# In the expert turns, each down unit is multiplied ahead of the transposes of the newest middle tile

## The chip, the core and the metric

The kernel runs on one core of a Trainium2 chip. Its time is the device time of one execution in microseconds (us), as the median of several runs. TensorE (PE in the rows) does the matrix products, its weight loads are shown apart as PEld, VectorE is DVE, ScalarE is ACT, GpSimd is POOL, and SyncE (SP) asks for the loads from HBM. Each engine works through its own instructions in the order in which they were written, and waits at an instruction until the semaphores that it names have come far enough.

## The reference, cut to what matters

The model is two hybrid blocks of two layers each over 256 tokens of width 1024. What the change touches is the last feed-forward part, a mixture of 8 experts with an inner width of 2816, two experts for each token:

```python
def _moe_swiglu(x, w_router, w_gate, w_up, w_down):
    ...
    top_logit, top_idx = lax.top_k(logits, TOP_K)
    top_w = jax.nn.softmax(top_logit, axis=-1)
    ...
    def expert_block(args):
        xs, e = args
        return (jax.nn.silu(xs @ w_gate[e]) * (xs @ w_up[e])) @ w_down[e]
    yb = lax.map(expert_block, (xb, block_expert))
    y_rows = yb.reshape(n_rows, d) * row_weight[:, None].astype(x.dtype)
    out = jnp.zeros_like(xf).at[row_token].add(y_rows)
```

All of it is float32, and the kernel keeps nearly that accuracy.

## The kernel before

**The whole.** Attention block, dense feed-forward, recurrent mixer and so on run first, up to 1510 us of the profiled execution. From there to 2361 us run the expert turns. One turn takes the up to 128 tokens of one expert through its three weight matrices. The program has a first turn written out, a loop of further turns and a last turn written out; with these inputs there are nine turns.

**The units.** An expert's weights come as 33 units of 1 MB, each 128 partitions by 2048 floats. The inner width is cut in 11 middle tiles of 256, j = 0 to 10. Tile j has three units: `near` j and `far` j (the halves of the gate and the up matrix over the model width) and `down` j. The order of the units in the stream is near j, far j, down j-2 for j = 2 to 10 (near and far alone for j = 0 and 1), then down 9 and down 10.

**The split.** A float32 product is made of three products in the faster rounded format. ScalarE copies a loaded unit into its high part (`w_hi`, line 1941), VectorE subtracts it from the unit to get the low part (`w_lo`, line 2962), and TensorE multiplies high by high, high by low and low by high. Each unit is 12 matmuls of 512 columns: line 1348 for near and far, line 1373 for down. A unit waits for its low part (`moe_lo`). High and low parts stand in four buffers, in three late in the turn; the raw units in six slots, later five. SyncE loads a slot anew once the low part of its last unit has been made.

**One middle tile.** When far j is done, ScalarE takes the silu of the gate half (line 1949) and VectorE multiplies it by the up half (line 2971, `moe_hidden`). TensorE then turns this 128 by 256 tile with two transposes (`turn_hidden`, line 1358, into bank 6). ScalarE copies the turned tile to its high part `hT_hi` (line 1924), and VectorE subtracts to get `hT_lo` (line 2956). `down` j needs both, two tiles later.

**What sets the order.** Four lists are written by hand, one for each engine, and share only semaphores. ScalarE and VectorE go through the units with an offset of two: step i makes the high part (VectorE: the low part) of unit i, and then does what belongs to unit i-2. In the step of far j ScalarE does this:

```python
act_(moe_part(w_hi, at), moe_slot(at), ACT.Copy)      # L1941, the unit near j+1
...
act_(act_m[:, j % 2, :], banks[4 + j % 2][:, 0:256], ACT.Silu)
if j:
    hT(j - 1)                                         # L1924; waits for turned_hidden j-1
```

The next high part in ScalarE's list, behind `hT(j-1)`, is that of far j+1, and then come those of down j-1 and near j+2. VectorE's list has the same sequence: hidden j, `hT_lo` j-1, and the low parts of far j+1, down j-1 and near j+2. Some small work of VectorE stands between `hT_lo` and the next low part (finding rows in the first turn, the picks of the next turn), and in the last turn rows of other turns are added (lines 2943 and 2947). Behind down 8 the turns but the last have eight transposes of gathered rows (line 1409), then `turn_hidden(10)`, down 9 and down 10; ScalarE and VectorE make the high and low part of down 10, the parts of the gathered rows, and then `hT` 10.

Of the kernel before, what the change touches and what calls it, by code (L numbers as in the profile page):

```python
# [217 lines left out]
def emit(nc, known, stream, par_d, cst_d, rows_d, x_d, out_d, n_stages):  # L218
# [5 lines left out]
    with ctx:  # L224
# [109 lines left out]
        def ct(name, i=0, n=None):  # L334
            a, w = CST.at[name]
            return cst[:, a + i:a + (w if n is None else i + n)]
# [3 lines left out]
        def sm(name, width):  # L340
            if name not in small_at:
                used = sum(w for _, w in small_at.values())
                assert used + width <= 512
                small_at[name] = (used, width)
            a, w = small_at[name]
            return small[:, a:a + w]
# [407 lines left out]
        def _(pe):  # L754
# [557 lines left out]
            if n_stages == 4:  # L1312
                mixer(1, MIX2_1)
                sel = sm("tables", 6 * 24).rearrange("p (t c) -> p t c", t=6)[:, 0:2, :]
                pe.wait_ge(*V.of("selected"))
                three = banks[1][:, 0:24].rearrange("p (t c) -> p t c", t=3)
                mm(three, ct("earlier"), sm("tables", 6 * 24).rearrange("p (t c) -> p t c", t=6)[:, 0:3, 0:8], start=True, stop=False)
                mm(three[:, 1:3, :], ct("ones"), grow(sel[:, 0, 0:8], [P, 2, 8], 1), start=False, stop=False)
                mm(three[:, 2, :], ct("ones"), sel[:, 1, 0:8], start=False, stop=True).then_inc(*T.done("places"))

                pe.wait_ge(*V.of("pick0"))
                for k in range(KT):
                    for tb in range(TB):
                        r = mm(banks[2 + k // 4][:, (k % 4) * P:(k % 4 + 1) * P], xr[:, tb, k * P:(k + 1) * P],
                               pick[:, tb, :], start=(tb == 0), stop=(tb == TB - 1))
                    if k % 4 == 3:
                        r.then_inc(*T.done("gather0", k // 4))

                def scatter(tb, half):

                    for y in (y_hi, y_lo):
                        r = mm(banks[2 + 4 * tb + half], pickT[:, tb * P:(tb + 1) * P], y[:, half * 512:(half + 1) * 512],
                               start=(y is y_hi), stop=(y is y_lo))
                    return r

                def turn(n, peeled, last=False):
                    where["turn"] = n

                    def up(kind, j):
                        i = MOE_UNIT[(kind, j)]  # L1340
                        if i >= 2:
                            pe.wait_ge(*V.of("moe_lo", i))
                        else:
                            pe.wait_ge(*(V.of("first_lo", i) if peeled else V.before("moe_lo", i)))
                        for q in range(4):
                            k = q + 4 * (kind == "far")
                            for a, b in ((xe_hi, w_hi), (xe_lo, w_hi), (xe_hi, w_lo)):
                                r = mm(banks[4 + j % 2], a[:, k, :], moe_part(b, i)[:, q * 512:(q + 1) * 512],  # L1348
                                       start=(k == 0 and a is xe_hi and b is w_hi), stop=(k == KT - 1 and b is w_lo))
                        r.then_inc(*T.done("moe_unit", i))  # L1350
                        T.same((f"moe_{kind}", j), ("moe_unit", i))

                    def turn_hidden(j):
                        pe.wait_ge(*V.of("moe_hidden", j))
                        if j:
                            pe.wait_ge(*V.of("hT", j - 1))
                        for c in range(2):
                            r = nc.tensor.transpose(banks[6][:, c * P:(c + 1) * P], hid_m[:, j % 2, c * P:(c + 1) * P],  # L1358
                                                    ct("ident"))
                        r.then_inc(*T.done("turned_hidden", j))  # L1360

                    def down(j):
                        i = MOE_UNIT[("down", j)]
                        pe.wait_ge(*V.of("moe_lo", i))
                        pe.wait_ge(*V.of("hT", j))
                        if j == 0:
                            pe.wait_ge(*A.of("y", 1))
                        order = [(c, half) for c in range(2) for half in range(2)]
                        if last and j == FJ - 1:
                            order = [(c, half) for half in range(2) for c in range(2)]  # L1370
                        for c, half in order:
                            for a, b in ((hT_hi, w_hi), (hT_lo, w_hi), (hT_hi, w_lo)):
                                r = mm(banks[half], a[:, j % 2, c * P:(c + 1) * P],  # L1373
                                       moe_part(b, i)[:, c * D + half * 512:c * D + (half + 1) * 512],
                                       start=(j == 0 and c == 0 and a is hT_hi and b is w_hi),
                                       stop=(j == FJ - 1 and c == 1 and b is w_lo))
                            if last and j == FJ - 1 and (c, half) == (1, 0):
                                r.then_inc(*T.done("last_half", 0))
                        r.then_inc(*T.done("moe_unit", i))
                        T.same(("last_half", 1), ("moe_unit", i))  # L1380
                        T.same(("moe_down", j), ("moe_unit", i))

                    for j in range(FJ):
                        if j == 0:
                            pe.wait_ge(*(V.of("xe0", 0) if peeled else V.before("xe", 0)))
                        elif j >= 2:
                            pe.wait_ge(*V.of("moe_hidden", j - 2))
                        up("near", j)
                        if j == 0:
                            pe.wait_ge(*(V.of("xe0", 1) if peeled else V.before("xe", 1)))  # L1390
                        up("far", j)
                        if j:
                            turn_hidden(j - 1)
                        if j >= 2:
                            down(j - 2)
                        if j == 8 and last:
                            pe.wait_ge(*V.of("pickw"))
                            for tb in range(TB):
                                r = nc.tensor.transpose(banks[7][:, tb * P:(tb + 1) * P], pickw[:, tb, :], ct("ident"))
                            r.then_inc(*T.done("pickT"))  # L1400
                        if j == 4 and not last:
                            pe.wait_ge(*V.of("pick"))
                            for tb in range(TB):
                                r = mm(banks[7][:, 256:257], pick[:, tb, :], ct("token", tb, 1), start=(tb == 0), stop=(tb == TB - 1))
                            r.then_inc(*T.done("row_at"))
                    if not last:
                        pe.wait_ge(s_gathered, n * 16 + 16)
                        for k in range(KT):
                            r = nc.tensor.transpose(banks[2 + k // 4][:, (k % 4) * P:(k % 4 + 1) * P],
                                                    turn_rows[:, k * P:(k + 1) * P], ct("ident"))  # L1410
                            if k % 4 == 3:
                                r.then_inc(*T.done("gather", k // 4))
                    turn_hidden(FJ - 1)
                    down(FJ - 2)
                    down(FJ - 1)
                T.enter()
                turn(0, True)
                T.again()
                load_turns(pe)
                with pe.Fori(1, where["turns"]) as n:  # L1420
                    turn(n, False)
                T.leave()
                turn(where["turns"], False, True)
                pe.wait_ge(*V.of("pickT"))
                for half in range(2):
                    pe.wait_ge(*V.of("last_y", half))
                    for tb in range(TB):
                        scatter(tb, half).then_inc(*T.done("last_scattered", tb, half))
# [1899 lines left out]
```

## Time and profile before

| what | value |
|---|---|
| median of 3 runs | 2379.02 us (2376.97 to 2379.52) |
| span of the profiled execution, first to last instruction | 2375.0 us |
| share of the span: PE, DVE, ACT | 98%, 81%, 61% |
| stretch of the expert turns, 1510 to 2351 us: PE busy | 840.4 of 841 us |
| same stretch: DVE, ACT busy | 744.8, 621.9 us |
| same stretch: mean busy share of the DMA engines | 0.97 |

The profiled execution's own time is its span plus what lies around it; the median of the runs is 4.0 us above the span. A busy share says how long an engine had an instruction in work, and not which engine waited for which. For that the timeline is read: each of its rows has the start in us from the span's start, the duration, the engine, the line, the operation and the tiles, how many instructions are merged in it (x), and in brackets how long the engine stood idle before it and what released it. TensorE's granted clock (PEclk) is 1.00 at 2.4 GHz and 0.50 at 1.2 GHz.

### The profile page before, as it was taken

The page shows a single profiled execution, that of the slowest core. Times are in us where ns is not written, and L with a number is a line of the kernel's source. Part 1 is how long each engine was busy: PE and PEld are TensorE (multiplying, and loading weights), DVE is VectorE, ACT ScalarE, POOL GpSimd, SP SyncE. Part 2 cuts the span into 40 slices and gives each one's busy share as a digit, 9 for nine tenths or more (in the row PEclk, how much of TensorE's full clock was granted, in tenths as well). Part 3 has the DMA queues.
Part 4 walks back from the last instruction along what each step waited for, and adds up shares of the span by engine and source line. Part 5 has one row for each costly group of instructions (what it writes and reads, how often), then busy time and mean ns, then how long its engine had stood idle before and what let it go on. Part 6 is the DMA issues. An engine that isn't in the chain of part 4 may idle for free.

```text
span 2375.0 us, 41596 instructions
## 1 busy us (share of the span) xinstructions
PE 2330.6 (98%) x16350; PEld 2040.7 (86%) x16350; DVE 1916.5 (81%) x2378; ACT 1442.3 (61%) x1765; POOL 139.3 (6%) x135
## 2 busy tenths in 40 slices
PE   8999999999999999999999999899999999999997
PEld 8998888999888999888889988788888888888886
DVE  5678877758888689876667887888888888888888
ACT  5765555665655553544446343677767777777775
POOL 2100000400000011100000120000000000000000
PEclk9999999999999999999999999899999999999999
DMA  6455553543655332455544223899999999999996
GB/s 236 162 195 195 195 195 125 189 167 136 224 188 193 141 143 91 161 195 192 189 164 173 108 91 124 343 362 385 384 367 393 361 382 392 359 385 386 368 381 267
DMA packets 83320, 575.23 MB, mean 242 GB/s; under 512 B 9568, under 2 KB 10080, under 8 KB 15840
## 3 DMA queue, kind: packets, MB, share of 16 engines
q1 hardware_dynamic: 78560, 554.21, 61.8%
q0 software_dynamic: 4608, 18.88, 2.0%
q8 instruction: 110, 1.80, 0.3%
q14 instruction: 42, 0.34, 0.0%
HBM read 561.25 MB, written 8.39 MB: 240 GB/s over the span
## 4 chain that ended last, share of the span: by engine, by line
PE 92%; DVE 4%; issue 2%; ACT 1%; DMA 0%; POOL 0%; DVEq 0%; SPq 0%; POOLq 0%; ACTq 0%
PE bank L1348 22%; PE bank L807 16%; PE bank L1373 11%; PE bank L816 9%; PE bank L854 7%; PE bank L818 5%; PE bank L909 4%; PE bank L888 3%; PE bank L1255 3%; PE bank L839 3%; DVE yT L2570 1%; PE bank L1358 1%; PE bank L1157 1%; PE bank L996 1%; DVE ring_lo L2492 0%
## 5 line engine op out<-in xcount | busy, mean ns | idle before, releaser
L2962 DVE TENSOR_TENSOR w_lo<-ring,w_hi 128x2048 fp32r<-128x2048 f32 x214 | 482.5, 2289 | 70.3 <-ACT w_hi L1941 69.0
L1941 ACT ACTIVATE w_hi<-ring 128x2048 fp32r<-128x2048 f32 x214 | 401.7, 1918 | 25.5 <-PE bank L1348 12.8
L1348 PE MATMUL bank<-w_hi,xe_hi 128*128 128x512 f32 x792 | 311.5, 393 | 0.5 <-DVE w_lo L2962 0.5
L1348 PE MATMUL bank<-w_lo,xe_hi 128*128 128x512 f32 x792 | 308.7, 390 | 0.0
L1348 PE MATMUL bank<-w_hi,xe_lo 128*128 128x512 f32 x792 | 308.2, 389 | 0.0
L2029 DVE TENSOR_TENSOR w_lo<-ring,w_hi 128x2048 fp32r<-128x2048 f32 x97 | 222.1, 2291 | 55.0 <-ACT w_hi L1478 53.6
L816 PE MATMUL bank<-x_both,w_hi 128*128 128x512 f32 x960 | 239.9, 392 | 0.0
L1478 ACT ACTIVATE w_hi<-ring 128x2048 fp32r<-128x2048 f32 x99 | 189.7, 1918 | 38.0 <-PE bank L854 34.1
L816 PEld LDWEIGHTS bank<-x_both,w_hi 128*128 128x128 f32 x960 | 174.3, 189 | 32.3
L1348 PEld LDWEIGHTS bank<-w_hi,xe_hi 128*128 128x128 f32 x792 | 148.7, 188 | 34.3 <-DVE w_lo L2962 4.3
L1348 PEld LDWEIGHTS bank<-w_lo,xe_hi 128*128 128x128 f32 x792 | 148.6, 188 | 31.5
L1348 PEld LDWEIGHTS bank<-w_hi,xe_lo 128*128 128x128 f32 x792 | 148.8, 188 | 30.1
L807 PE MATMUL bank<-x_hi,in_hi 128*128 128x256 f32 x576 | 164.3, 285 | 0.0
L1373 PE MATMUL bank<-w_hi,hT_hi 128*128 128x512 f32 x396 | 163.8, 414 | 0.3 <-DVE w_lo L2962 0.2
L807 PE MATMUL bank<-x_hi,ring_lo 128*128 128x256 f32 x576 | 162.3, 282 | 0.0
L807 PE MATMUL bank<-x_lo,in_hi 128*128 128x256 f32 x576 | 161.3, 280 | 0.0
L2156 DVE TENSOR_TENSOR ring_lo<-ring,in_hi 128x2048 fp32r<-128x2048 f32 x39 | 89.4, 2295 | 85.2 <-ACT in_hi L1517 85.1
L1489 ACT ACTIVATE gates<-bank 128x256 f32<-128x256 f32 x120 | 39.6, 382 | 191.4 <-PE bank L818 191.4
L1373 PE MATMUL bank<-w_hi,hT_lo 128*128 128x512 f32 x396 | 155.6, 393 | 0.0
L1373 PE MATMUL bank<-w_lo,hT_hi 128*128 128x512 f32 x396 | 155.0, 391 | 0.0
L1949 ACT ACTIVATE gates<-bank 128x256 f32<-128x256 f32 x99 | 38.0, 384 | 175.6 <-PE bank L1348 175.0
L818 PEld LDWEIGHTS bank<-x_both,w_lo 128*128 128x128 f32 x960 | 131.0, 190 | 9.4
(468 smaller groups left out, 5833.5 us busy)
## 6 DMA issues: line engine op xcount, KB each, us to landing
ring<-in_stream SPq DMA_DIRECT2D x431, 1024.0 KB, 5.4
yT<-in_stream SPq DMA_DIRECT2D x54, 1024.0 KB, 7.7
xT<-in_stream SPq DMA_DIRECT2D x27, 1024.0 KB
Z<-in_stream SPq DMA_DIRECT2D x8, 1024.0 KB, 7.7
norm_rows<-in_rows POOLq DMA_DIRECT2D x4, 1024.0 KB, 7.3
slot_rows<-gates POOLq DMA_DIRECT2D x8, 512.0 KB, 8.9
Z<-Z SPq DMA_DIRECT2D x24, 128.0 KB, 2.1
slot_rows<-cst POOLq DMA_DIRECT2D x4, 512.0 KB, 4.2
```

What stands on the lines that cost most here:

```text
L807: r = mm(bank[:, c * SEQ:(c + 1) * SEQ], w[a][:, at], x[b][:, k, :], start=(k == 0 and a == b), stop=(k == KT - 1 and a == 1))
L816: mm(two[c], w[0][:, at[k]], x_both[:, :, k, :], start=(k == 0), stop=False)
L818: r = mm(two[c][:, SEQ:2 * SEQ], w[1][:, at[k]], x_hi[:, k, :], start=False, stop=(k == KT - 1))
L854: r = mm(banks[2 * tb + half], a[:, j % 2, c, tb * P:(tb + 1) * P], part(b, n)[:, c * D + half * 512:c * D + (half + 1) * 512], start=(j = ...
L909: r = mm(banks[2 * tb + half], g[a], w[:, c, half * 512:(half + 1) * 512], start=(n == 0 and c == 0 and a == b), stop=(n == 3 and c == 1 a ...
L1348: r = mm(banks[4 + j % 2], a[:, k, :], moe_part(b, i)[:, q * 512:(q + 1) * 512], start=(k == 0 and a is xe_hi and b is w_hi), stop=(k == K ...
L1373: r = mm(banks[half], a[:, j % 2, c * P:(c + 1) * P], moe_part(b, i)[:, c * D + half * 512:c * D + (half + 1) * 512], start=(j == 0 and c ...
L1478: act_(part(w_hi, n), slot(f0 + n), ACT.Copy).then_inc(*A.done("hi", f0 + n))
L1941: act_(moe_part(w_hi, at), moe_slot(at), ACT.Copy).then_inc(*A.done("moe_hi", at))
L2029: v.tensor_tensor(part(w_lo, n), slot(f0 + n), part(w_hi, n).bitcast(F32), ALU.subtract)\
L2156: v.tensor_tensor(slot_lo(u), slot(u), hi.bitcast(F32), ALU.subtract).then_inc(*V.done("lo", u))
L2962: v.tensor_tensor(moe_part(w_lo, at), moe_slot(at), moe_part(w_hi, at).bitcast(F32), ALU.subtract)\
```

## The change

In `turn`, for each j from 2 to 10, `down(j - 2)` is called ahead of `turn_hidden(j - 1)` instead of behind it. The number of instructions and the waits that each one carries stay the same.

```diff
                         up("far", j)
+                        if j >= 2:
+                            down(j - 2)
                         if j:
                             turn_hidden(j - 1)
-                        if j >= 2:
-                            down(j - 2)
```

TensorE at j = 2 of the first turn, before. Bank 4 is that of far 2, bank 6 takes the transposes, banks 0 and 1 sum the down units, and bank 5 is that of near 3:

```order
L1348 MATMUL bank4<-w_hi_49,xe_lo_96 128x512
L1348 MATMUL bank4<-w_lo_50,xe_hi_95 128x512
L1358 MATMUL bank6<-cst,gates 128x128 x2
L1373 MATMUL bank0<-w_hi_49,hT_hi_97 128x512
...
L1373 MATMUL bank1<-w_hi_49,hT_hi_97 128x512
L1373 MATMUL bank1<-w_hi_49,hT_lo_98 128x512
L1373 MATMUL bank1<-w_lo_50,hT_hi_97 128x512
L1348 MATMUL bank5<-w_hi_3_54,xe_hi_95 128x512
```

The same place in the changed kernel:

```order
L1348 MATMUL bank4<-w_hi_49,xe_lo_96 128x512
L1348 MATMUL bank4<-w_lo_50,xe_hi_95 128x512
L1373 MATMUL bank0<-w_hi_49,hT_hi_97 128x512
L1373 MATMUL bank0<-w_hi_49,hT_lo_98 128x512
...
L1373 MATMUL bank1<-w_hi_49,hT_lo_98 128x512
L1373 MATMUL bank1<-w_lo_50,hT_hi_97 128x512
L1358 MATMUL bank6<-cst,gates 128x128 x2
L1348 MATMUL bank5<-w_hi_3_54,xe_hi_95 128x512
```

The two transposes moved behind the 12 matmuls of down 0, directly in front of near 3. ScalarE's list is the same in both kernels. Around the copies of turned tiles 1 and 2 it reads (`gates<-bank` is the silu, `hT_hi` the copy of the turned tile):

```order
L1949 ACTIVATE gates<-bank4 128x256
L1924 ACTIVATE hT_hi_97<-bank6 128x256
L1941 ACTIVATE w_hi_49<-ring 128x2048 x2
L1941 ACTIVATE w_hi_49<-yT 128x2048
L1949 ACTIVATE gates<-bank5 128x256
L1924 ACTIVATE hT_hi_97<-bank6 128x256
L1941 ACTIVATE w_hi_3_54<-xT 128x2048
```

The first `w_hi` behind each `hT_hi` is the high part of a far unit: far 3 behind the first, far 4 (from xT) behind the second. Nothing moved here, nor on VectorE, GpSimd or SyncE.

At the end of a turn that is not the last, TensorE reads before:

```order
L1373 MATMUL bank1<-w_lo_50,hT_hi_97 128x512
L1409 MATMUL bank2<-cst,Z 128x128 x4
L1409 MATMUL bank3<-cst,Z 128x128 x4
L1358 MATMUL bank6<-cst,gates 128x128 x2
L1373 MATMUL bank0<-w_hi_49,hT_hi_97 128x512
```

and in the changed kernel:

```order
L1373 MATMUL bank1<-w_lo_50,hT_hi_97 128x512
L1358 MATMUL bank6<-cst,gates 128x128 x2
L1409 MATMUL bank2<-cst,Z 128x128 x4
L1409 MATMUL bank3<-cst,Z 128x128 x4
L1358 MATMUL bank6<-cst,gates 128x128 x2
L1373 MATMUL bank0<-w_hi_49,hT_hi_97 128x512
```

The transposes of tile 9 moved behind down 8, in front of those of the gathered rows.

## Rows read from the trace of the kernel before

**Rows 1.** The page: the span, and the chain that ended last, by engine.

```profile
span 2375.0 us, 41596 instructions
...
PE 92%; DVE 4%; issue 2%; ACT 1%; DMA 0%; POOL 0%; DVEq 0%; SPq 0%; POOLq 0%; ACTq 0%
```

**Rows 2.** Groups by line, 1450 to 2375 us: the transposes of line 1358.

```profile
L1358 PE MATMUL bank<-cst,gates 128*128 128x128 f32 x198 | 37.6, 271 | 0.0
```

**Rows 3.** Waits, 1510 to 2351 us: total us, times, longest.

```profile
ACT gates L1949 <- PE bank L1348: 174.2, 94, 2.9
...
PEld bank L1348 <- DVE w_lo L2962: 4.3, 13, 0.7
```

**Rows 4.** Timeline of TensorE, second turn: transposes, down, near, far, transposes.

```profile
1629.71 0.38 PE L1358 MATMUL bank<-cst,gates 128*128 128x128 f32 x2
1629.85 0.47 PE L1373 MATMUL bank<-w_hi,hT_hi 128*128 128x512 f32 x1
...
1632.70 0.39 PE L1348 MATMUL bank<-w_hi,xe_hi 128*128 128x512 f32 x1
...
1635.42 0.39 PE L1348 MATMUL bank<-w_hi,xe_hi 128*128 128x512 f32 x1
...
1638.14 0.38 PE L1358 MATMUL bank<-cst,gates 128*128 128x128 f32 x2
```

**Rows 5.** Timeline of ScalarE, same stretch: silu, hT, first high part.

```profile
1629.99 0.38 ACT L1949 ACTIVATE gates<-bank 128x256 f32<-128x256 f32 x1 [2.37 <-PE bank L1348]
1630.27 0.38 ACT L1924 ACTIVATE hT_hi<-bank 128x256 fp32r<-128x256 f32 x1
1630.53 1.92 ACT L1941 ACTIVATE w_hi<-xT 128x2048 fp32r<-128x2048 f32 x1
```

**Rows 6.** Timeline of VectorE, same stretch: the three low parts.

```profile
1632.49 2.29 DVE L2962 TENSOR_TENSOR w_lo<-xT,w_hi 128x2048 fp32r<-128x2048 f32 x1 [1.09 <-ACT w_hi L1941]
1634.70 4.49 DVE L2962 TENSOR_TENSOR w_lo<-ring,w_hi 128x2048 fp32r<-128x2048 f32 x2
```

**Rows 7.** Timeline of three engines, end of the last turn.

```profile
2349.91 4.49 DVE L2962 TENSOR_TENSOR w_lo<-ring,w_hi 128x2048 fp32r<-128x2048 f32 x2
...
2352.25 0.50 PE L1373 MATMUL bank<-w_hi,hT_hi 128*128 128x512 f32 x1 [0.17 <-DVE w_lo L2962]
...
2355.12 0.44 PE L1358 MATMUL bank<-cst,gates 128*128 128x128 f32 x2
...
2355.67 0.38 ACT L1924 ACTIVATE hT_hi<-bank 128x256 fp32r<-128x256 f32 x1 [0.82 <-PE bank L1358]
```

**Rows 8.** Timeline, end of the second turn: transposes 9, down 10's start; VectorE.

```profile
1689.26 0.38 PE L1358 MATMUL bank<-cst,gates 128*128 128x128 f32 x2
...
1696.13 0.40 PE L1373 MATMUL bank<-w_hi,hT_hi 128*128 128x512 f32 x1
...
1692.04 2.29 DVE L2962 TENSOR_TENSOR w_lo<-yT,w_hi 128x2048 fp32r<-128x2048 f32 x1 [0.39 <-ACT w_hi L1941]
...
1695.45 0.41 DVE L2956 TENSOR_TENSOR hT_lo<-bank,hT_hi 128x256 fp32r<-128x256 f32 x1
```

**Rows 9.** Timeline of TensorE before the turns: three waits of over 2 us.

```profile
1229.16 1.76 PE L765 MATMUL bank<-cst,xres 128*128 128x128 f32 x8 [2.44 <-DVE xres L2414]
...
1454.15 0.36 PE L888 MATMUL bank<-branch_hi,proj_hi 128*128 128x256 f32 x1 [2.08 <-DVE branch_lo L2766]
...
1492.69 1.92 PE L1303 MATMUL bank<-par,xT 128*128 128x8 f32 x16 [2.30 <-DVE xT L1992]
```

**Rows 10.** Windows: length, busy us (instructions) of PE to POOL, PEclk, DMA share, GB/s.

```profile
1230.00:1232.00 2.00, 1.72 (x9) 1.35 (x8) 2.00 (x5) 1.22 (x4) 0.01 (x1) 0.50 0.00 0
...
1454.00:1462.00 8.00, 7.85 (x53) 7.88 (x54) 7.69 (x11) 2.73 (x3) 0.00 (x0) 0.79 0.45 172
1455.00:1458.00 3.00, 3.00 (x16) 3.00 (x16) 3.00 (x6) 1.91 (x1) 0.00 (x0) 0.50 0.82 317
1459.00:1462.00 3.00, 3.00 (x27) 3.00 (x27) 2.69 (x3) 0.17 (x1) 0.00 (x0) 1.00 0.00 0
...
1492.00:1494.00 2.00, 1.31 (x12) 1.34 (x13) 1.66 (x4) 0.04 (x1) 0.56 (x1) 1.00 1.04 434
1510.00:2351.00 841.00, 840.39 (x3822) 688.71 (x3821) 744.79 (x554) 621.92 (x529) 19.02 (x20) 1.00 0.97 376
```

## The prediction

> **What bounds the kernel now.** I read the page first, then the waits of the expert turns, then the timelines of three engines over one middle tile. The reader is to see that the chain which ended last is 92% TensorE [rows 1], and that in the 841 us of the turns TensorE is busy for 840.4 at full clock [rows 10]. Its waits there are trifles: 4.3 us in all for low parts, never over 0.7 us [rows 3]. So in this stretch any time that TensorE loses anew is lost to the span. The others look free: ScalarE stands 174.2 us waiting for far units before its silu, 2.37 us of it in the tile shown [rows 3, 5], and VectorE is idle for 1.09 us before the first low part [rows 6]. The DMA engines have a mean share of 0.97 [rows 10], so there is no spare bandwidth for anything faster than now; the change asks for no more bytes.
>
> A share tells nothing of the distance between a low part and its use, and that is what counts here. In the tile shown the low part of the far unit runs from 1632.49 for 2.29 us, to 1634.78 [rows 6]. TensorE starts that far unit at 1635.42 [rows 4]. The margin is 0.64 us.
>
> **The change, part by part.** Nothing is removed or added: the same two transposes and 12 matmuls swap places, so TensorE's own work is unchanged. The gain that it could bring is that down never stands behind a wait of the transposes. Transposes have an idle of 0.0 us over all 198 [rows 2], so that gain is nothing. The other thing the move does is to delay the transposes by one down unit. Before, from the first transpose to the first near matmul are 1632.70 - 1629.71 = 2.99 us, of which 0.14 is the transposes [rows 4]; 2.85 us is down's share, and of this 0.1 is the slower restart behind transposes (0.47 against 0.39 us for the first), which near then has instead. The transposes come 2.75 us later.
>
> Who waits for them: ScalarE's copy of the turned tile. Behind that copy in ScalarE's list are the high parts of far j+1, down j-1 and near j+2, and behind those high parts VectorE's low parts, and behind the low part of far j+1 TensorE itself. ScalarE's idle time doesn't help, because it lies before the silu, ahead of the copy, and not between the copy and the low part.
>
> The chain from the first transpose's start (call it 0), each link from a row:
> - transposes end and the copy starts: 2355.67 - 2355.12 = 0.55 with transposes of 0.44 [rows 7]; with the usual 0.38 [rows 4] it is 0.49;
> - copy to first high part: 1630.53 - 1630.27 = 0.26 [rows 5];
> - high part to its low part: 1632.49 - 1630.53 = 1.96 [rows 5, 6];
> - low part: 2.29 [rows 6];
> - low part to the matmul that waits for it: the first of two low parts ends at 2349.91 + 2.29 = 2352.20, the matmul starts at 2352.25, so 0.05 [rows 7].
>
> The sum is 5.05 us. In the changed kernel TensorE has only the transposes and near j+1 to do meanwhile: 0.14 + 0.1 + 2.72 (1635.42 - 1632.70) [rows 4] = 2.96, so it waits 2.1 us before far j+1. It is the same as the delay of 2.75 less the margin of 0.64. The first matmul after a wait takes 0.50 instead of 0.39 [rows 7], 0.1 more. I take **2.2 us** for each tile.
>
> Is it paid once or at every tile? Every time: the next transposes stand behind far j+1 and down j-1, so TensorE's delay moves them too, and the chain closes on itself. The period was 1638.14 - 1629.71 = 8.43 us [rows 4] and becomes about 10.6. What else is in the period stays hidden. The three low parts start at 2.72, 4.93 and 7.13 (each 2.21 after the one before, from 1632.49 and 1634.70 [rows 6]); that of down j-1 ends at 7.2, needed at 5.05 + 2.8 = 7.9; that of near j+2 at 9.4, needed at 10.8. ScalarE has 6.5 us of work in it, VectorE 7.7. The small work of VectorE behind `hT_lo` was covered by 1.09 us of idle [rows 6] and has about the same now. SyncE's loads wait for the same low parts, now 2.2 us further apart each tile, so the bytes per us fall and loads land earlier against their use; no DMA queue is passed. The bound on this from below is 0 (the loads weren't the limit), and above 4.3 us of old waits saved.
>
> Which tiles: the transposes of tiles 1 to 8 are moved and have a far unit behind (far 3 to 10), so 8 waits in a turn. 198 transposes in pairs over 11 tiles are 9 turns [rows 2]. 8 x 9 x 2.2 = **158 us**.
>
> The transposes of tile 9 have no far unit behind; there the chain goes through ScalarE to down 10. VectorE's low part of down 10 started at 1692.04 and `hT_lo` 10 ended at 1695.45 + 0.41 = 1695.86, 3.82 later, with the gathered rows between [rows 8]. Now the low part starts at 0.49 + 0.26 + 1.96 = 2.71 behind the transposes; `hT_lo` ends at 6.53, and down 10 starts at 6.6. Before, down 10 started 1696.13 - 1689.26 = 6.87 after the transposes [rows 8]; the transposes are 2.75 later, so it is 9.35 against 6.87, and with the 0.1 of restart 2.6 us. Eight turns make **21 us**. In the last turn no rows are gathered; the same chain without the 1.2 us of their low parts (1695.45 - 1692.04 less one low part's 2.21) costs about 2 us.
>
> Sum of the waits: 158 + 21 + 2 = **181 us**.
>
> **The clock.** A wait of over 2 us comes in TensorE every 10.6 us. Three rows show such a wait outside the turns. After 2.08 us (at 1454.15) the clock was 0.50 from 1455 to 1458, after 2.44 us (at 1229.16) it was 0.50 at 1230, and after 2.30 us (at 1492.69) it was still 1.00 up to 1494 [rows 9, 10]. So a wait of this size can bring a fall from 2.4 to 1.2 GHz, and doesn't always. Price of one fall: over 1454 to 1462 the mean clock was 0.79, so 0.21 x 8 / 0.5 = 3.4 us at half clock; in 3 us of it 16 matmuls ran, in 3 us at full clock 27 [rows 10], which is 41% lost, or 1.4 us. It lies in far or down, thus on the chain. With 81 waits the bounds are 0 and, with a fall at each, 113 us; two in three would be 76. The work on both sides of these waits is denser than at any of the three places, 8.4 us of 512 columns without a gap, so I take the lower part: one in four, 20 x 1.4 = **28 us**.
>
> The Trainium skill ("TensorE: Matmul & The Clock Gate", HAM oscillation) puts the danger only at idle gaps longer than these; by it there is no fall, and the sum would stay at 181. The trace speaks against it at 1454.15, where the gap was 2.08 us and the clock fell, so its case is kept as a rival and not as the forecast.
>
> Total: the profiled span of 2375.0 [rows 1] becomes 2375.0 + 181 + 28 = 2584, and the median of the runs, 4.0 above the span now, 2588 us.
>
> **Rivals.**
> 1. *The waits come, the clock holds.* For it: the dense work around each wait, and the place at 1492.69. Against: the other two places. 2375 + 181 + 4 = 2560 us.
> 2. *The clock falls at nearly each wait.* For it: two of three places. Against: each place shown came after thinner work too. 2560 + 113 = 2673 us.
> 3. *The wait is paid once a turn.* After the first late far unit ScalarE and VectorE might run ahead, since their busy time is below TensorE's. Then 9 x (2.2 + 2.6) = 43 us, 2422 us. Against: the high part of each far unit is behind a copy that is itself behind the whole of TensorE's list up to there; running ahead isn't possible.
> 4. *Not slower.* ScalarE's 2.37 us of idle before the silu and VectorE's 1.09 [rows 5, 6] swallow the 2.75, and the time stays at 2379. It decides at the margin of the low part of far j+1: this must be 2.75 us or more, and the rows show 0.64. It would need the high part of far j+1 to stand ahead of the copy in ScalarE's list, which it doesn't.
>
> **How the numbers follow.** Forecast 2588 (waits and some falls): 0.56. Rival 1: 0.28. Rival 2: 0.07. Rival 3: 0.04. Rival 4: 0.03, and 0.02 for something that I don't see. The range takes in rival 1 with 0.15 us less at each of 81 waits (12 us), 2548, and above the falls at about six in ten waits (70 us), 2632; that leaves out rivals 2 to 4 and a little of the ends. A measurement of this kernel tells 0.2% (4.8 us) from no change. Slower by more: 0.96. Within: 0.02. Faster: 0.02.
>
> **What would show it.** In the waits, TensorE (or its weight loads) for `w_lo` of line 2962 before line 1348, 72 times, about 2.1 us each, 150 us in all, and 8 or 9 waits of 2 to 2.5 us before line 1373 at down 10. Transposes to transposes 10.6 us instead of 8.43. ScalarE's wait for line 1348 before the silu shrinks from 2.37 to about 1.5 us, and a wait for line 1358 before the copy of about 2.8 us appears. The DMA share falls from 0.97 to about 0.8. Granted clock in the turns below 1.00: with 20 falls, 68 us at half of some 1020, 0.97. I am wrong on the mechanism if the waits stand before near or down and not before far, or if there are 9 of them and not 72; and on the clock term if the granted clock stays at 1.00 or is below 0.92.

## The result and the profile after

The changed kernel takes 2583.55 us (median of 4 runs, 2580.05 to 2584.95) against 2378.64 us for the kernel before in the same session (2376.97 to 2379.52). The ratio is 1.0858, 95% interval 1.0843 to 1.0874: 204.9 us slower. Predicted were 2588 us.

The page of the changed kernel, the span and the chain by engine:

```profile
span 2580.8 us, 41596 instructions
...
PE 79%; DVE 10%; ACT 7%; issue 3%; ACTq 0%; DMA 0%; POOL 0%; DVEq 0%; SPq 0%; POOLq 0%
```

The chain was 92% TensorE and 5% VectorE and ScalarE [rows 1]. Now 17% of it lies on those two: the chain runs through them once per tile. The waits of the turns, 1510 to 2560 us (total us, times, longest):

```profile
ACT hT_hi L1924 <- PE bank L1358: 205.9, 81, 3.2
ACT gates L1949 <- PE bank L1348: 174.1, 93, 3.5
PEld bank L1348 <- DVE w_lo L2962: 161.8, 78, 3.2
...
PE bank L1348 <- DVE w_lo L2962: 129.7, 72, 2.8
...
PE bank L1373 <- DVE hT_lo L2956: 16.1, 8, 2.0
```

The weight loads waited 4.3 us in all for low parts [rows 3]; now it is 161.8 us (weight loads overlap the matmuls, so this is not to be added to the next figure). TensorE's own 129.7 us are in exactly 72 waits, one for each far unit behind moved transposes, and the 8 waits before line 1373 are those at the ends of the turns but the last. ScalarE's copy now waits 81 times for the transposes. One tile on TensorE (second turn; transposes, first far matmul, transposes), and the same on ScalarE (the copy, the high parts, the next silu) and VectorE:

```profile
1650.07 0.38 PE L1358 MATMUL bank<-cst,gates 128*128 128x128 f32 x2
1655.06 0.50 PE L1348 MATMUL bank<-w_hi,xe_hi 128*128 128x512 f32 x1 [1.82 <-DVE w_lo L2962]
1660.63 0.38 PE L1358 MATMUL bank<-cst,gates 128*128 128x128 f32 x2
```

```profile
1650.49 0.38 ACT L1924 ACTIVATE hT_hi<-bank 128x256 fp32r<-128x256 f32 x1 [2.48 <-PE bank L1358]
1650.77 3.70 ACT L1941 ACTIVATE w_hi<-ring 128x2048 fp32r<-128x2048 f32 x2
...
1658.18 0.38 ACT L1949 ACTIVATE gates<-bank 128x256 f32<-128x256 f32 x1 [1.90 <-PE bank L1348]
```

```profile
1652.71 4.50 DVE L2962 TENSOR_TENSOR w_lo<-ring,w_hi 128x2048 fp32r<-128x2048 f32 x2 [0.87 <-ACT w_hi L1941]
```

From the transposes at 1650.07 the copy is 0.42 away, the high part 0.28 more, the low part 1.94 more, and far starts 2.35 after that: 4.99 us in all. The bracket of 1.82 is less than the 2.1 us of the prediction, since it counts from the modelled end of the last near matmul and not from when the next could have started. The period is 10.56 us; it was 8.43 [rows 4].

The granted clock in windows (columns as in rows 10; the first two lie in the first turn, the last is the whole of the turns):

```profile
1538.00:1541.00 3.00, 3.00 (x8) 2.31 (x7) 3.00 (x2) 0.00 (x0) 0.00 (x0) 0.50 0.90 366
1550.00:1560.00 10.00, 8.52 (x41) 6.81 (x40) 7.42 (x10) 5.54 (x6) 0.00 (x0) 1.00 0.78 308
1510.00:2557.00 1047.00, 899.87 (x3847) 709.50 (x3846) 754.21 (x567) 625.07 (x531) 21.11 (x20) 0.97 0.80 305
```

Behind the wait before far that ended at 1536.65 the clock stood at 0.50 through the window of 1538 to 1541. The window from 1550 also has waits of this kind on both sides, and full clock. The mean fell from 1.00 to 0.97 and the DMA share from 0.97 to 0.80. The records of the clock hold 20 stretches at half clock in the turns, each of 3.4 us. In the periods from transposes to transposes they stand out: up to the last turn tiles last 10.56 to 10.63 us, or 12.2 where the clock fell, as in the first of these two:

```profile
1681.84 0.38 PE L1358 MATMUL bank<-cst,gates 128*128 128x128 f32 x2
...
1694.05 0.38 PE L1358 MATMUL bank<-cst,gates 128*128 128x128 f32 x2
...
1704.61 0.38 PE L1358 MATMUL bank<-cst,gates 128*128 128x128 f32 x2
```

### The profile page after: what moved, and what is told of

Its sections match the earlier page's. It is cut to its first block, busy times and chain, and to the rows that moved or that the text cites. A ratio compares the mean times of both kernels' runs of the same rounds, so it can differ in the third digit from the quotient of the medians.

```text
span 2580.8 us, 41596 instructions
## 1 busy us (share of the span) xinstructions
PE 2387.8 (93%) x16350; PEld 2059.4 (80%) x16350; DVE 1920.9 (74%) x2378; ACT 1445.0 (56%) x1765; POOL 141.3 (5%) x135
## 4 chain that ended last, share of the span: by engine, by line
PE 79%; DVE 10%; ACT 7%; issue 3%; ACTq 0%; DMA 0%; POOL 0%; DVEq 0%; SPq 0%; POOLq 0%
PE bank L807 15%; PE bank L1348 14%; PE bank L1373 10%; PE bank L816 8%; PE bank L854 7%; DVE w_lo L2962 6%; ACT w_hi L1941 6%; PE bank L818 4%; PE bank L909 3%; PE bank L1255 3%; PE bank L888 3%; PE bank L839 2%; PE bank L1358 1%; DVE yT L2570 1%; PE bank L1157 1%
## 5 line engine op out<-in xcount | busy, mean ns | idle before, releaser
L1348 PE MATMUL bank<-w_hi,xe_hi 128*128 128x512 f32 x792 | 333.2, 421 | 129.7 <-DVE w_lo L2962 129.7
L1348 PE MATMUL bank<-w_hi,xe_lo 128*128 128x512 f32 x792 | 317.7, 401 | 0.0
L1348 PE MATMUL bank<-w_lo,xe_hi 128*128 128x512 f32 x792 | 317.1, 400 | 0.0
L1348 PEld LDWEIGHTS bank<-w_hi,xe_hi 128*128 128x128 f32 x792 | 151.7, 192 | 189.8 <-DVE w_lo L2962 161.8
L2956 DVE TENSOR_TENSOR hT_lo<-bank,hT_hi 128x256 fp32r<-128x256 f32 x99 | 41.9, 424 | 150.2 <-ACT hT_hi L1924 150.2
L1924 ACT ACTIVATE hT_hi<-bank 128x256 fp32r<-128x256 f32 x99 | 38.1, 385 | 205.9 <-PE bank L1358 205.9
L1489 ACT ACTIVATE gates<-bank 128x256 f32<-128x256 f32 x120 | 39.6, 382 | 191.2 <-PE bank L818 191.2
```

## The experiments

Each kernel was compared with the kernel before in its own session (medians of 2378.7 to 2379.7 us). The question: is the loss the chain through ScalarE's and VectorE's lists, or something of TensorE's new order, the clock or the loads?

**1. `lists_moved`: the chain is cut.** TensorE as in the changed kernel. In the two other lists the copy and the low part of turned tile j-1 go behind the parts of far j+1.

```diff
 # ScalarE and VectorE, in the step of far j
-                            if j:
-                                hT(j - 1)
+                            if j == 1:
+                                hT(0)
 # in the step of down j, behind the high (VectorE: low) part of far j+3
+                        if kind == "down" and j <= FJ - 3:
+                            hT(j + 1)
```

> TensorE as in the changed kernel; in ScalarE's and VectorE's lists the copy and the low part of turned tile j-1 stand behind the high and low part of far j+1 instead of ahead of them (tiles 1 to 9). Theory: the loss is the chain transposes, hT, high part, low part, far. With far's parts ahead of hT the chain is cut, the waits before line 1348 go (under 10 us in all), the clock stays at 1.00 and the time is that of before, 2379 us within 5. Rival, TensorE's own new order costs the time (the down unit directly behind far, or the clock): it stays near 2583 us.

Measured: 2393.55 us, ratio 1.0063 (1.0046 to 1.008). Of 205 us, 190 are gone; the rival is out. But 14.5 us remained, more than expected. TensorE's waits in the turns:

```profile
PE bank L1358 <- DVE hT_lo L2958: 11.4, 9, 1.8
PE bank L1373 <- DVE w_lo L2964: 1.8, 3, 0.8
PE bank L1348 <- DVE w_lo L2964: 0.7, 2, 0.5
```

The waits before line 1348 are gone, as expected. There are nine new ones before the transposes: at the end of a turn `hT_lo` 9 now stands behind the low part of down 10, and transposes 10 wait for it. The edit had moved a wait.

**2. `lists_tiles`: the same without tile 9.**

```diff
 # ScalarE and VectorE, against lists_moved
-                            if j == 1:
-                                hT(0)
+                            if j in (1, FJ - 1):
+                                hT(j - 1)
 # ...
-                        if kind == "down" and j <= FJ - 3:
+                        if kind == "down" and j < FJ - 3:
                             hT(j + 1)
 # TensorE; for j = 10 down stays behind turn_hidden
-                        if j >= 2:
+                        if 2 <= j < FJ - 1:
                             down(j - 2)
```

> As lists_moved, but only for tiles 1 to 8; tile 9 stands on all engines as in the kernel before. Theory: what lists_moved still lost, 14.5 us, is the wait of transposes 10 for hT_lo 9, which stands there behind the low part of down 10 (11.4 us of waits in nine turns). Without it nothing is left of the loss: 2379 us within 4, though TensorE's order is the changed one in 8 of 9 tiles. Rival, the new order of TensorE costs something of its own at each tile: 2390 us or more.

Measured: 2380.89 us, ratio 1.0006 (0.9997 to 1.0016), no difference from before that this measurement can tell. The transposes of tile 0 in the second and third turn, in the kernel before and then here:

```profile
1615.56 0.38 PE L1358 MATMUL bank<-cst,gates 128*128 128x128 f32 x2
...
1709.93 0.38 PE L1358 MATMUL bank<-cst,gates 128*128 128x128 f32 x2
```

```profile
1618.47 0.38 PE L1358 MATMUL bank<-cst,gates 128*128 128x128 f32 x2
...
1712.77 0.38 PE L1358 MATMUL bank<-cst,gates 128*128 128x128 f32 x2
```

A turn lasts 94.30 us here against 94.37 before. TensorE's changed order costs nothing at these tiles once the other two lists fit it; only the last turn, from its first transposes to the end of the span, is 1.9 us longer (100.8 against 98.9).

**3. `scalar_moved` and 4. `vector_moved`: one list each.** The edit of `lists_moved` on one engine alone.

> The changed kernel with only ScalarE's list altered: far's high part ahead of the copy hT, for tiles 1 to 9. VectorE still makes hT_lo ahead of far's low part. Theory: the chain loses its link of 1.96 us and becomes 0.49 to the copy, 0.41 to hT_lo, 0.35 to the low part, 2.29, 0.05 = 3.6 us against 2.96 of TensorE's work; 0.65 us a tile, 47 us, the ends some 9, and the small work of VectorE that is now on the chain some 7: 2442 us. Rival, ScalarE's list alone is the cause: 2393 us as lists_moved. Rival, it has to be both or nothing: 2583.

Measured: 2439.97 us, ratio 1.0255 (1.0238 to 1.0272). The period by the rows is 9.09 us, the expected 8.43 + 0.65:

```profile
1681.54 0.38 PE L1358 MATMUL bank<-cst,gates 128*128 128x128 f32 x2
1685.05 0.50 PE L1348 MATMUL bank<-w_hi,xe_hi 128*128 128x512 f32 x1 [0.35 <-DVE w_lo L2964]
1690.63 0.38 PE L1358 MATMUL bank<-cst,gates 128*128 128x128 f32 x2
```

From transposes to far are 3.51 us instead of 4.99: the high part's link is out of the chain, that of `hT_lo` has come in.

> The changed kernel with only VectorE's list altered: far's low part ahead of hT_lo, for tiles 1 to 9. Theory: the chain goes through ScalarE as before (copy, high part, low part), so the tiles lose the same; at the end hT_lo 9 is behind the low part of down 10 and transposes 10 wait for it, 1.7 us more a turn: 2598 us. Rival, hT_lo in front of the low part is the cause: under 2500 us.

Measured: 2616.63 us, ratio 1.0996 (1.0971 to 1.102). The tiles lose what they lost (period 10.56). The total is 19 us above the expectation. TensorE's waits:

```profile
PE bank L1348 <- DVE w_lo L2962: 129.9, 72, 2.8
PE bank L1358 <- DVE hT_lo L2956: 37.5, 9, 4.9
```

The 129.9 us before line 1348 are those of the changed kernel. The nine waits before the transposes are 4.2 us each on average, and behind each of them the clock fell, at seven for 6.8 us instead of 3.4. There are 26 stretches at half clock in the turns, 17 of them in the tiles against 13 in the changed kernel. The price of the longer falls and of those added was missing in the expectation.

**5. `six_ahead` and 6. `three_ahead`: how the loss depends on the delay.** The transposes stand inside the down unit, behind 6 or 3 of its 12 matmuls.

```diff
 # down(j, first, end) now makes only the matmuls from first up to end
                         if j >= 2:
-                            down(j - 2)
+                            down(j - 2, 0, 6)          # three_ahead: 0, 3
                         if j:
                             turn_hidden(j - 1)
+                        if j >= 2:
+                            down(j - 2, 6, 12)         # three_ahead: 3, 12
```

> The transposes stand in the middle of the down unit, behind its first 6 matmuls instead of behind all 12. They come 6 x 0.23 = 1.4 us later than before. Theory: each tile loses the delay less the margin of 0.64, plus 0.1 for the restart, 0.85 us: 72 x 0.85 = 61, and the ends 9 x 1.25 = 11, together 72 us, 2451 us, with no falls of the clock. Rival, the loss is proportional to the delay, without a margin: half of 205 us, 2481 us. Rival, any down matmul ahead costs all: 2583 us.

> The transposes stand behind the first 3 matmuls of down, 0.68 us later than before. Six ahead lost 0.77 us a tile for a delay of 1.37, all lost 2.12 for 2.72, so the loss is the delay less 0.60. Theory: 0.08 x 72 = 6 us, the ends 9 x (0.68 - 0.25) = 4, together 2389 us. Rival, proportional from zero (a quarter of 205 us): 2430 us.

Measured: 2442.09 us, ratio 1.0269 (1.0251 to 1.0286), and 2390.7 us, ratio 1.0047 (1.003 to 1.0064). The first transposes of the second turn in `six_ahead`, and the next two:

```profile
1625.04 0.38 PE L1358 MATMUL bank<-cst,gates 128*128 128x128 f32 x2
...
1632.11 0.38 PE L1358 MATMUL bank<-cst,gates 128*128 128x128 f32 x2
...
1641.31 0.38 PE L1358 MATMUL bank<-cst,gates 128*128 128x128 f32 x2
```

The first interval of a turn has the delay in it and no wait yet; the next is the period. The four kernels read in this way, in the steady part of a turn:

| down matmuls ahead | transposes later by, us | period, us | loss for a tile, us | time above before, us |
|---|---|---|---|---|
| 0 | 0 | 8.44 | 0 | 0 |
| 3 | 0.68 | 8.53 | 0.09 | 12 |
| 6 | 1.37 | 9.20 | 0.76 | 63 |
| 12 | 2.72 | 10.56 | 2.12 | 205 |

The delay is the first interval of a turn (7.07 us in the rows above) less the 5.70 us of before. From 3 to 12 the loss grows one for one with the delay, and the line meets zero at 0.6 us, which is the margin of 0.64 from [rows 4, 6]. Proportional it isn't. The last column has the ends and, at 12, the clock in it too. Six ahead had no fall of the clock in the turns, with waits of 0.5 us by the bracket.

**7. `end_only` and 8. `tiles_only`: the two parts alone.**

```diff
 # for the other j, down stays behind turn_hidden
-                        if j >= 2:
+                        if j == FJ - 1:          # tiles_only: 2 <= j < FJ - 1
                             down(j - 2)
```

> Only the transposes of tile 9 are moved (behind down 8); tiles 1 to 8 as before. Theory: 8 turns at 2.5 us and the last at 2, some 22 us, so 2401 us, up to 2405 with a few falls of the clock; TensorE waits for hT_lo before down 10. Rival, the next turn's slack gives it back: 2379 us.

> Only the transposes of tiles 1 to 8 are moved, those of tile 9 as before. Theory: the two parts add up. The ends cost 30 us by end_only, so 2583.5 - 30 = 2553 us, of which some 13 falls of the clock at 1.6 us. Rival, the end's loss was partly the tiles' loss seen again: above 2565 us.

Measured: 2409.16 us, ratio 1.013 (1.0113 to 1.0147), and 2549.15 us, ratio 1.0712 (1.0694 to 1.073). They cost 30 and 169.5 us, together 199.6 of the 204.9. The clock fell 6 times in the turns of the first and 11 times in those of the second, against 20 in the changed kernel: three falls at 1.6 us each (the price is worked out under 9) are the missing 5 us. TensorE's waits in the first:

```profile
PE bank L1373 <- DVE hT_lo L2958: 17.0, 9, 2.0
```

(eight of about 2.0 us, and one of 0.8 in the last turn) and the end of its first turn, the transposes 9 and 10 and the first matmul of down 10:

```profile
1598.31 0.38 PE L1358 MATMUL bank<-cst,gates 128*128 128x128 f32 x2
1599.71 0.41 PE L1358 MATMUL bank<-cst,gates 128*128 128x128 f32 x2 [0.15 <-DVE hT_lo L2958]
1604.91 0.64 PE L1373 MATMUL bank<-w_hi,hT_hi 128*128 128x512 f32 x1 [2.05 <-DVE hT_lo L2958]
```

Down 10 starts 6.60 us behind transposes 9, and in the prediction 6.6. The end costs 2.5 us a turn where the clock held (turns of 96.84 against 94.37 us) and 4.1 where it fell (98.45). It fell at 6 of the 8 ends with such a wait, more often than expected, hence 30 us and not 22 to 26.

**9. `wait_filled` and 10. `filled_before`: the clock's share.** TensorE gets work to do in its wait.

```diff
                         for q in range(4):
                             k = q + 4 * (kind == "far")
+                            if kind == "near" and j >= 3 and q == 3:
+                                for _ in range(7):
+                                    mm(banks[3], xe_hi[:, k, :], moe_part(w_hi, i)[:, q * 512:(q + 1) * 512], start=True, stop=True)
```

> The changed kernel with 7 matmuls of 512 columns more in each near unit of tiles 3 to 10 (their result in bank 3 is used by nothing), 1.6 us that stand where TensorE waits 2.1 us for the low part of far. Theory: the chain is not lengthened, the waits shrink to 0.5 us, the granted clock in the turns is 1.00 but for the turns' ends, and the time falls by the cost of the falls, from 2583 to about 2558 us, although 115 us of TensorE work are added. Rival, the falls of the clock cost nothing because they lie in other waits: 2583 us. If near were on the chain: 2698 us.

> The kernel before with the same 7 matmuls of 512 columns more in each near unit of tiles 3 to 10 (their result is used by nothing). Theory: there is no wait there for them to stand in, so all 9 x 8 x 7 = 504 of them lengthen the span, 0.227 us each, 114 us: 2493 us. Rival, such extra matmuls are cheap anywhere, and the 25 us gained by wait_filled say nothing of waits: under 2420 us.

Measured: 2558.01 us, ratio 1.0751 (1.0733 to 1.0769), which is 25.5 us faster than the changed kernel with 504 matmuls more; and 2490.99 us, ratio 1.0469 (1.0452 to 1.0487), which is 111.3 us slower than before with the same 504. So 0.221 us each where there is no wait, and nothing where there is one. One tile of `wait_filled` (line 1351 is here far's matmul, 1361 the transposes):

```profile
1648.67 0.38 PE L1361 MATMUL bank<-cst,gates 128*128 128x128 f32 x2
1653.66 0.50 PE L1351 MATMUL bank<-w_hi,xe_hi 128*128 128x512 f32 x1 [0.25 <-DVE w_lo L2965]
1659.23 0.38 PE L1361 MATMUL bank<-cst,gates 128*128 128x128 f32 x2
```

From transposes to far are 4.99 us and the period is 10.56, both as in the changed kernel, with the wait down from 1.82 to 0.25. Only the falls are fewer: none is left in the tiles, where there were 13, and 4 in place of 7 at the turns' ends, where nothing was filled in. If the 16 falls that are gone account for the 25.5 us, each cost 1.6 us, as the periods of 12.2 against 10.6 us say too.

**11. `lists_on_before`: a wider margin without the swap.** TensorE as before, the lists of `lists_tiles`.

> TensorE as in the kernel before, ScalarE's and VectorE's lists as in lists_tiles: the margin of far's low part grows from 0.64 to over 2 us. Theory: TensorE was busy for 840.4 of 841 us, so a wider margin is worth only the small waits of before, 0 to 4 us: 2375 to 2379 us. Rival, the margin of 0.64 was costing time in some turns: 2370 us or less.

Measured: 2379.22 us, ratio 0.9997 (0.9988 to 1.0007): no difference. The margin that was there was enough. None of these versions beats the kernel before.

## Why the prediction was right, point by point

**The chain and its links.** Right, and shown by more than the time. Far starts 4.99 us behind the transposes against 5.05 worked out. Taking out ScalarE's link changes the period as its length says (3), VectorE's list alone changes nothing in the period (4), both together cut the chain (1, 2).

**Paid at every tile.** Right: 72 waits of like size, and a constant period. The rival of one payment a turn (43 us) is out.

**2.2 us for each tile.** Slightly high: 2.12. The restart of 0.1 us was taken rightly: before, down had it behind the transposes; now far has it behind its wait, and from far's start to the next transposes are 5.57 us in the new rows (1655.06 to 1660.63) as from far's start over down in the old ones (2.72 and 2.85). What is over is the chain, 5.05 us for 4.99. Its first link, from the transposes to the copy, was taken from the end of the last turn as 0.49 us and is 0.42 in the tiles. At the tile that has the small products of `row_at` (four matmuls of one column, line 1404) the period was 8.94 and became 10.6, so the loss there is 1.65: 0.5 us of TensorE's work went under cover of the wait. I had not seen that. Seven tiles of 2.12 and one of 1.65 are 16.5 a turn, 148 us in nine, in place of 158. (The last turn has no such tile; it was counted like the others.)

**The ends.** 2.5 us measured against 2.6 in the turns but the last, and 2.2 in the last against 2 (`end_only`, from the last turn's first transposes to the end of the span).

**The clock.** The term that rested on three rows came out nearly right. The number of falls was 20, as taken, but that was a choice between bounds and no result, so the agreement is luck: 13 of them are in tiles (of 72) and 7 at ends (of the 8 with a wait of 2.0 us), so it wasn't one in four everywhere. `tiles_only` has 11 at the same 72 waits. Each cost 1.6 us and not 1.4: a period with a fall is 12.18 against 10.57. The price had come from a place with 256 columns. That is 32 us for 28. The rule of the Trainium skill ("TensorE: Matmul & The Clock Gate", HAM oscillation), which puts the danger at idle gaps longer than these, does not hold here: gaps of 1.8 us by the bracket were followed by half clock, though never at all of them. The first rival, waits without falls, gave 2560; `wait_filled` is nearly that kernel and measures 2558.

**The sum.** The waits are 148 + 8 x 2.5 + about 2 = 170, the falls 20 x 1.6 = 32, together 202; the profiled spans differ by 205.8 and the medians by 204.9. The transposes of tile 0 in the first turn, before anything that was changed, stand here in the kernel before and in the changed one:

```profile
1521.23 0.38 PE L1358 MATMUL bank<-cst,gates 128*128 128x128 f32 x2
```

```profile
1523.26 0.38 PE L1358 MATMUL bank<-cst,gates 128*128 128x128 f32 x2
```

So 2.0 of the 205.8 us lie ahead of the turns and are no effect of the change (at this place the 13 profiled executions of this case differ by up to 5 us). From there on the difference is 203.8 us, 1.8 more than the sum. The forecast had 181 and 28, together 209: the waits 11 us too high, the clock 4 us too low, so part of the closeness is that two errors go against each other.

**What the other engines' idle time was worth.** ScalarE waits 174.1 us before its silu, as much as before [rows 3], and 205.9 us more before the copy. Here the signs of the prediction were off: the wait before the silu was to shrink to about 1.5 us and is 1.90 in the rows shown, and the one before the copy is 2.48 and not 2.8. Its idle time was no reserve, because it lay on the wrong side of the instruction that was delayed. The rival on the other side rested on it, and failed as its own condition said.

**The loads.** Not in the way: the DMA share is down to 0.80, the period is constant with different slots in use, and in the list of waits of the turns only one, of 1.1 us on ScalarE, is for a load.

## What to carry to other kernels

When an instruction is moved on one engine, look in every other engine's list for what stands behind the instruction that waits for it: the loss is the delay less the smallest margin on that path, paid each time that the path closes on itself, here once per tile. Moving an instruction in one list means moving its consumers in the others too; with both lists changed the same order on TensorE cost nothing. And in this kernel a recurring wait of about 2 us on TensorE had a second price, the clock, which could be read apart by giving it work to do in the wait.

## What the runs showed that was not expected

Added work made a kernel faster: 504 matmuls of 512 columns in the waits took 25.5 us off the time of the changed kernel, since they kept the clock at 2.4 GHz in the tiles. The kernel before is still 179 us faster.

The clock fell much oftener at waits that have thin work beside them. At the ends, with a wait of 2.0 us and transposes and gathered rows shortly before it, it fell at 7 of 8; at the tiles, with a wait of 1.8 us between dense units, at 13 of 72; behind the waits of 4.2 us in `vector_moved`, in all nine turns. How much of this is the wait's length and how much the work beside it, no run tells apart. The waits of 0.5 us in the tiles and 0.9 at the ends (`six_ahead`), and of 1.2 us at the ends (`lists_moved`), had none.

And neither of the two settles a single case. Ahead of the turns all 13 kernels are alike, and TensorE has a wait of 2.08 us before line 888 that the three of [rows 9] leave out. Here it is in the kernel before and in `six_ahead`, each with a window behind it:

```profile
1005.53 0.35 PE L888 MATMUL bank<-branch_hi,proj_hi 128*128 128x256 f32 x1 [2.08 <-DVE branch_lo L2766]
1005.50:1012.00 6.50, 6.47 (x55) 6.50 (x56) 6.50 (x9) 1.92 (x1) 0.00 (x0) 1.00 0.52 203
```

```profile
1006.66 0.55 PE L888 MATMUL bank<-branch_hi,proj_hi 128*128 128x256 f32 x1 [2.08 <-DVE branch_lo L2775]
1006.70:1009.70 3.00, 3.00 (x14) 3.00 (x15) 3.00 (x6) 1.31 (x1) 0.00 (x0) 0.50 0.96 339
```

Behind the same wait, among the same instructions, the clock held in the first and fell in the second. Over the 13 profiled executions it fell here in 5, and in 11 at the wait of 2.08 us at 1454.15 [rows 9]. What decides it stays open.
